# An expert's accumulating transfers by column blocks into four tables, and small constants made later

## What is computed

```python
def moe(xn, w_router, wg, wu, wd):
    ...
    top_vals, top_idx = lax.top_k(logits, TOP_K)
    gates = jax.nn.softmax(top_vals, axis=-1)
    comb = jnp.einsum('nk,nke->ne', gates, jax.nn.one_hot(top_idx, N_EXPERTS, dtype=jnp.float32))
    y = jnp.zeros_like(t)
    for e in range(N_EXPERTS):
        y = y + comb[:, e:e + 1].astype(t.dtype) * swiglu(t, wg[e], wu[e], wd[e])
    return y.reshape(B, S, D)
```

## Time and profile before

| | |
|---|---|
| runs, median | 1997.23 us |
| runs, lowest and highest | 1994.70 and 1999.85 us |
| the profiled execution | 1999.13 us |
| its span in the profile | 1997.2 us, mean granted clock 0.986 |
| TensorE busy | 1936.9 us (97%) |
| VectorE busy | 1358.9 us (68%) |
| ScalarE busy | 1182.9 us (59%) |
| POOL busy | 99.3 us (5%) |
| DMA | 513.45 MB, mean 257 GB/s |

### The profile page before, as it was taken

One profiled execution on the slowest core, in us unless ns is written; L12 is line 12 of the kernel. 1 busy time (PEld: TensorE's weight loads), 2 busy tenths in 40 slices (PEclk: granted clock), 3 DMA queues, 4 the chain that ended last, 5 costly groups with the idle time before them and its releaser, 6 DMA issues.

```text
span 1997.2 us, 27157 instructions
## 1 busy us (share of the span) xinstructions
PE 1936.9 (97%) x9170; PEld 1614.0 (81%) x9170; DVE 1358.9 (68%) x1616; ACT 1182.9 (59%) x1501; POOL 99.3 (5%) x126
## 2 busy tenths in 40 slices
PE   9889999999999999999998989999999999999998
PEld 8778888888888888888887878878787878787876
DVE  8666654544554454546666668889798979788887
ACT  7666543434434343435555657878687878777775
POOL 8300000000000000000200000000000000000000
PEclk9999999999999999999998989999999999999999
DMA  9444566666566666666654459999999999999996
GB/s 353 145 134 149 178 189 186 192 193 189 185 190 190 190 190 191 191 187 186 188 168 135 160 201 363 364 382 366 376 363 379 362 379 360 381 359 385 354 392 256
DMA packets 139251, 513.45 MB, mean 257 GB/s; under 512 B 15648, under 2 KB 15664, under 8 KB 136464
## 3 DMA queue, kind: packets, MB, share of 16 engines
q1 hardware_dynamic: 135440, 488.74, 70.7%
q0 software_dynamic: 3712, 23.44, 4.0%
HBM read 497.43 MB, written 14.69 MB: 256 GB/s over the span
## 4 chain that ended last, share of the span: by engine, by line
PE 82%; DMA 7%; ACT 3%; DVE 3%; POOL 2%; issue 2%; SPq 0%; ACTq 0%; DVEq 0%; POOLq 0%
PE main L599 26%; PE main L601 25%; PE main L600 25%; DMA raw_pieces<-in_ffn_moe 7%; ACT w_high L1031 1%; DVE w_low L1364 1%; PE transpose L927 1%; PE transpose L970 1%; PE transpose L617 1%; PE transpose L798 0%; PE transpose L910 0%; PE spread L661 0%; DVE heads_scratch L1412 0%; DVE small L1413 0%; PE transpose L639 0%
## 5 line engine op out<-in xcount | busy, mean ns | idle before, releaser
L1364 DVE TENSOR_TENSOR w_low<-raw_pieces,w_high 128x1024 fp32r<-128x1024 f32 x919 | 1095.5, 1225 | 469.4 <-ACT w_high L1031 465.1
L1031 ACT ACTIVATE w_high<-raw_pieces 128x1024 fp32r<-128x1024 f32 x919 | 944.9, 1058 | 280.5 <-DMA raw_pieces<-in_ffn_moe 142.2
L599 PE MATMUL main<-w_high,xT_high 128*128 128x512 f32 (+1 forms) x1920 | 738.1, 384 | 1.4 <-DVE x_resid L1562 1.0
L601 PE MATMUL main<-w_high,xT_low 128*128 128x512 f32 (+1 forms) x1920 | 725.8, 378 | 0.0
L600 PE MATMUL main<-w_low,xT_high 128*128 128x512 f32 (+1 forms) x1920 | 725.5, 378 | 0.0
L601 PEld LDWEIGHTS main<-w_high,xT_low 128*128 128x128 f32 x1920 | 364.6, 190 | 67.9
L599 PEld LDWEIGHTS main<-w_high,xT_high 128*128 128x128 f32 x1920 | 366.0, 191 | 65.7 <-issue 2.4
L600 PEld LDWEIGHTS main<-w_low,xT_high 128*128 128x128 f32 x1920 | 365.7, 190 | 63.7
L599 PE MATMUL main<-w_high,hT_high 128*128 128x512 f32 x832 | 329.2, 396 | 0.7 <-DVE hT_low L1771 0.7
L601 PE MATMUL main<-w_high,hT_low 128*128 128x512 f32 x832 | 324.6, 390 | 0.0
L600 PE MATMUL main<-w_low,hT_high 128*128 128x512 f32 x832 | 324.2, 390 | 0.0
(11 more groups left out here) (248 smaller groups left out, 883.8 us busy)
## 6 DMA issues: line engine op xcount, KB each, us to landing
raw_pieces<-in_ffn_moe SPq DMA_DIRECT2D x528, 512.0 KB, 5.6
raw_pieces<-in_ffn_dense SPq DMA_DIRECT2D x264, 512.0 KB, 3.7
raw_pieces<-in_w_in SPq DMA_DIRECT2D x96, 512.0 KB, 3.7
raw_pieces<-in_w_out SPq DMA_DIRECT2D x32, 512.0 KB, 3.6
residual_rows<-x_resid POOLq DMA_DIRECT2D x3, 1024.0 KB, 6.2
x_resid<-in_x SPq DMA_DIRECT2D x4, 512.0 KB, 14.7
xn_rows<-token_major POOLq DMA_DIRECT2D x2, 1024.0 KB, 5.1
x_resid<-residual_rows POOLq DMA_DIRECT2D x4, 512.0 KB, 7.6
```

What stands on the lines that cost most here:

```text
L599: pe.matmul(out_ap, lh[ls], rh[rs], start=first, stop=False)
L601: return pe.matmul(out_ap, ll[ls], rh[rs], start=False, stop=last)
L1031: act.activation(WH[:, piece % RING, :], RAWS[:, piece % RING, :], ACT.Copy).then_inc(high_done, 1)
L1364: dve.tensor_tensor(WL[:, piece % RING, :], RAWS[:, piece % RING, :], WH[:, piece % RING, :], ALU.subtract).then_inc(low_done, 1)
```

## The change

Two parts. The table becomes four tables of 384 x 512, one for each column block, with a semaphore each, and the one accumulating transfer of an expert becomes four, each issued when its block of `Y` is done. The table's first filling goes by columns as well (4 writes of 512 KB and 4 of 256 KB in place of 3 of 1 MB), and the gathers no longer wait for `y_out`. VectorE's wait at step 8 is for all four semaphores. The second part takes the eight small instructions of `TOKEN`, `PLACE` and `VAL` out of `masks()` and puts them behind `rope_tables(0)`.

```diff
-        RESULTS = nc.dram_tensor("residual_rows", (SEQ + SLOTS, D), F32, kind="Internal").ap()
+        RESULTS = [nc.dram_tensor(f"residual_rows{d}", (SEQ + SLOTS, NB), F32, kind="Internal").ap() for d in range(DBLOCKS)]
...
-        x_out, y_out = sem("residual_stored"), sem("y_out")
+        x_out, y_out = sem("residual_stored"), [sem(f"y_out{d}") for d in range(DBLOCKS)]
...
             def masks():
                 link(pool.tensor_copy(IOTA[:, :], IOTA_I))
-                pool.wait_ge(token_iota, 2)
-                link(pool.tensor_copy(TOKEN[:, :], TOKEN_I[:, :]))
-                link(pool.tensor_copy(PLACE[:, 0:1], PLACE_I[:, :]))
-                link(pool.tensor_scalar(PLACE[:, 1:2], PLACE[:, 0:1], -1.0, None, ALU.mult))
-                link(pool.tensor_scalar(PLACE[:, 2:3], PLACE[:, 0:1], float(SEQ), None, ALU.add))
-                for t in range(TILES):
-                    link(pool.memset(VAL[:, t, 2, :], 1.0))
-                    ins = pool.tensor_scalar(VAL[:, t, 0, :], VAL[:, t, 2, :], TOKEN[:, t:t + 1], None, ALU.mult)
-                ins.then_inc(token_done, 1)
                 link(pool.tensor_copy(DF, DIST))
...
             rope_tables(0)
 
+            pool.wait_ge(token_iota, 2)
+            link(pool.tensor_copy(TOKEN[:, :], TOKEN_I[:, :]))
...
+            ins.then_inc(token_done, 1)
+
             pool.wait_ge(used, MIX[1]["piece"])
...
             pool.wait_ge(dn_free, FFN[1]["dn"])
-            for t in range(TILES):
-                pool.dma_start(RESULTS[t * P:(t + 1) * P, :], X[:, t, :]).then_inc(x_out, 16)
-            pool.dma_start(RESULTS[SEQ:SEQ + SLOTS, :], X[:, 0, :]).then_inc(y_out, 16)
-            pool.wait_ge(x_out, 16 * TILES)
-            pool.wait_ge(y_out, 16)
+            for d in range(DBLOCKS):
+                pool.dma_start(RESULTS[d][0:SEQ, :].rearrange("(t p) n -> p t n", p=P),
+                               X[:, :, d * NB:(d + 1) * NB]).then_inc(x_out, 16)
+            for d in range(DBLOCKS):
+                cols = slice(d * NB, (d + 1) * NB)
+                pool.dma_start(RESULTS[d][SEQ:SEQ + SLOTS, :], X[:, 0, cols]).then_inc(y_out[d], 16)
+            pool.wait_ge(x_out, 16 * DBLOCKS)
             for e in range(N_EXP - 1):
                 pool.wait_ge(idx_done, e + 2)
                 pool.indirect_dma_start(XG, None, ROWS[:, :], bass.IndirectOffsetOnAxis(ap=IDX[:, 0:1], axis=0)).then_inc(xg_in, 16)
 
 
-                pool.wait_ge(y_out, 16 * e + 16)
                 pool.wait_ge(cur_done, e + 1)
-                pool.wait_ge(dn_free, PASS[0]["dn"] + DBLOCKS * (e + 1))
-                pool.indirect_dma_start(RESULTS[:, :], bass.IndirectOffsetOnAxis(ap=RC[:, 0:1], axis=0), Y, None,
-                                         compute_op=ALU.add).then_inc(y_out, 16)
+                for d in range(DBLOCKS):
+                    cols = slice(d * NB, (d + 1) * NB)
+                    pool.wait_ge(y_out[d], 16 * e + 16)
+                    pool.wait_ge(dn_free, PASS[0]["dn"] + DBLOCKS * e + d + 1)
+                    pool.indirect_dma_start(RESULTS[d][:, :], bass.IndirectOffsetOnAxis(ap=RC[:, 0:1], axis=0), Y[:, cols], None,
+                                            compute_op=ALU.add).then_inc(y_out[d], 16)
...
-            pool.wait_ge(y_out, 16 * N_EXP)
+            for d in range(DBLOCKS):
+                pool.wait_ge(y_out[d], 16 * N_EXP)
...
                         if i == E_SELECT and not direct:
 
-                            dve.wait_ge(y_out, e * 16 + 16)
+                            for d in range(DBLOCKS):
+                                dve.wait_ge(y_out[d], e * 16 + 16)
                             dve.tensor_copy(GC[:, :], GN[:, :])
```

More of the change, by code:

```diff
@@ L548, in _ @@
             rope_tables(0)
+            pool.wait_ge(token_iota, 2)
+            link(pool.tensor_copy(TOKEN[:, :], TOKEN_I[:, :]))
+            link(pool.tensor_copy(PLACE[:, 0:1], PLACE_I[:, :]))
+            link(pool.tensor_scalar(PLACE[:, 1:2], PLACE[:, 0:1], -1.0, None, ALU.mult))
+            link(pool.tensor_scalar(PLACE[:, 2:3], PLACE[:, 0:1], float(SEQ), None, ALU.add))
+            for t in range(TILES):
+                link(pool.memset(VAL[:, t, 2, :], 1.0))
+                ins = pool.tensor_scalar(VAL[:, t, 0, :], VAL[:, t, 2, :], TOKEN[:, t:t + 1], None, ALU.mult)
+            ins.then_inc(token_done, 1)
             pool.wait_ge(used, MIX[1]["piece"])
@@ L591, in _ @@
                 pool.dma_start(X[:, :, d * NB:(d + 1) * NB],
-                               RESULTS[0:SEQ, d * NB:(d + 1) * NB].rearrange("(t p) n -> p t n", p=P)).then_inc(back_in[d], 16)
+                               RESULTS[d][0:SEQ, :].rearrange("(t p) n -> p t n", p=P)).then_inc(back_in[d], 16)
         @block.tensor
```

## The result

The changed kernel takes 1963.14 us, the median of four runs (1961.98 to 1965.02); the kernel before, run beside it, takes 1996.01 (1994.70 to 1999.85). The ratio is 0.9833 with a 95% interval from 0.9816 to 0.9850: 33 us less (29.9 to 36.7). The forecast was 1969.0 with a range from 1964 to 1988, so the sign is right, the gain is 4 us more than the 29.2 of the sum, and the time is 0.9 us outside the range.

A forecast was written before the change was run, and what follows sets the result against it. TensorE was taken to set the pace, stalling once per expert when one late 1 MB accumulating transfer delays weights. Savings 18.0 + 8.3 + 2.9 = 29.2 us from 1999.13 give 1969.9, from the median 1968.0; forecast 1969, range 1964 to 1988.

The forecast's parts named there:

- slow stretches: Experts: after six of the gaps TensorE runs at its lower clock; removing these saves 6 x 1.38 = 8.3 us.
- seven gaps, 18.0 us: Experts, second onward: TensorE's stalls of 2.15 to 3.11 us before the first transpose all go, saving 18.0 us.
- The experts as a whole: Experts: gaps and slow stretches together were forecast to save 26.3 us.
- The small constants: Kernel start: moving eight instructions shortens POOL's chain before ScalarE's sine; all 2.9 us comes through, bounds 2.4 and 2.9.
- small gaps of 0.48 us: Last transpose of an expert: left in the forecast; if gone too, 7 x 0.48 = 3.4 us toward the range's lower end.
- Lag and cover: First transpose of the next expert: weights' lag of 0.3 to 1.3 us stays inside 1.2 to 2.2 us covered by pieces made ahead.
- Rival (a): Experts: gaps stay in part, through leftover lag or smaller packets alternating with weights; gain 13 to 21 us, 1978 to 1986; 18%.
- 92.3 us, with 2.8 us to spare: One expert's DMA work: pieces 84.2, gather 2.8, four quarters 5.3 us, fitting within 95.1 us.
- POOL's issues and the filling: POOL: 21 more issues and five more table-filling issues, 1.71 us each, fit in its idle time and cost nothing.
- The rule against the change: Experts' transfers: if the skill's 2.0 us fixed per DMA filled the engines, four cost 10.4 us against 4.4 for one.
- rival (c): Experts: each transfer's fixed time fills the DMA engines; 2033 us, or 1993 by the skill's fit; 3%.

The follow-up runs named there:

- 1: Kernel before with only the eight small instructions moved behind the rope tables; 1992.54 us, ratio 0.9978 to the kernel before.
- 2: Changed kernel with the eight small instructions put back into `masks()`, leaving four tables and four transfers alone; 1969.59 us, ratio 0.9868 to the kernel before.
- 5: Changed kernel run again, unaltered; 1962.91 us, ratio 0.9826 to the kernel before.
- 9: Changed kernel without the move of the small constants, run a second time; 1969.16 us, ratio 0.9859 to the kernel before.
- 4: Kernel before without the seven accumulating transfers, first seven experts' results left out of the sum; 1967.58 us, ratio 0.9858 to the kernel before.
- 3: Changed kernel with each of the four transfers waiting for the expert's last block; 1982.18 us, ratio 0.9930 to the kernel before.
- 6: Changed kernel with two tables of 1024 columns and two transfers, after the second and fourth block; 1972.73 us, ratio 0.9876 to the kernel before.
- 7: Changed kernel with each expert's last quarter accumulated a second time, into a spare table; 1973.24 us, ratio 0.9884 to the kernel before.
- 11: Changed kernel with all four quarters of each expert accumulated a second time, into a spare table; 2012.64 us, ratio 1.0076 to the kernel before.
- 12: Changed kernel with two transfers of half the columns, both after the last block; 1993.52 us, ratio 0.9990 to the kernel before.
- experiment 10: Changed kernel with POOL's two small loads (frequencies, positions) issued in the middle of `masks()`; 1961.81 us, ratio 0.9830 to the kernel before.
- experiment 8: Changed kernel with POOL's angles and their loads ahead of the rest of `masks()`; 1969.16 us, ratio 0.9859 to the kernel before.

## Why the prediction was right, and where it was not

**The gaps and the slow stretches: right, the second a little small.** The step "seven gaps, 18.0 us" measured 18.1, from 23.5 to 5.4 us of idle time. The experts as a whole gave 27.4 us: to the end of the span they take 807.9 to 810.1 us with the old transfer (before, 1) and 780.4 to 782.2 with four (changed, 2, 5, 9), means 809.0 and 781.6; by the ratios of 2 and 9 it is 26.3 and 28.1. Forecast 26.3. The slow stretches were then worth 27.4 - 18.1 = 9.3 us for 8.3 forecast, if all that remains is put down to them.

**The small constants: the step that failed.** The term "all of it comes through: 2.9" with bounds 2.4 and 2.9 measured 4.4 alone and 6.8 beside the four transfers. The wait before the sine fell as forecast, from 5.43 to 2.45, and the sine came 2.9 us earlier (52.39 to 49.47). But the experts start 5.1 us earlier: at 1185.2 us in the mean of four kernels with the constants unmoved (before, 2, 4, 9: 1183.7 to 1187.1), at 1180.1 in the mean of eight with them moved and nothing else changed at the start (changed, 1, 3, 5, 6, 7, 11, 12: 1177.1 to 1182.5). From the scatter of these twelve starts the 5.1 is known to some 2.6 us. 27.4 + 5.1 = 32.5 us, where 32.9 were measured.

The other 2.2 us go with the granted clock of the mixers. Half of them are there early: TensorE's first transpose of `h_blocks` in the dense part of layer 0 stands at 255.2 us in the mean of the four and at 251.2 in that of the eight, 4.0 us earlier. Where the lead grows from 2.9 to 4.0 shows in the 12 us from 60 on, for the kernel before, the changed kernel and the changed kernel again (the clock is the third number from the end):

```profile
60.00:72.00 12.00, 6.40 (x26) 5.31 (x26) 7.92 (x10) 6.18 (x10) 7.09 (x11) 0.86 0.26 67
```

```profile
60.00:72.00 12.00, 9.81 (x40) 7.75 (x40) 5.69 (x7) 7.45 (x11) 6.96 (x15) 0.86 0.35 113
```

```profile
60.00:72.00 12.00, 9.72 (x46) 7.86 (x45) 7.15 (x10) 9.03 (x13) 7.25 (x15) 1.00 0.44 141
```

With the constants unmoved TensorE waits 4.75 to 5.60 us just before, and the clock of these 12 us is 0.72 to 0.86 in all four. With them moved it waits at most 2.48 us, and the clock is 0.86 in four kernels (changed, 1, 3, 6) and 1.00 in the other four (5, 7, 11, 12). The same kernel shows both, so a gap of this length is followed by the lower clock in some executions and not in others. The later stages differ as well. Two stretches of each, of the kernel before and then of the changed one:

```profile
1050.00:1100.00 50.00, 43.96 (x194) 36.14 (x193) 33.10 (x56) 28.11 (x40) 0.00 (x0) 0.90 0.43 128
1150.00:1200.00 50.00, 44.09 (x257) 37.79 (x257) 33.63 (x79) 28.49 (x56) 2.65 (x5) 0.90 0.55 200
```

```profile
1050.00:1100.00 50.00, 45.29 (x216) 37.77 (x217) 35.44 (x63) 27.23 (x38) 0.00 (x0) 0.97 0.44 134
1150.00:1200.00 50.00, 44.09 (x263) 37.79 (x262) 35.31 (x77) 29.48 (x55) 6.10 (x10) 0.93 0.60 213
```

Of the stretches of 50 us that I read, from 55 to 305 and from 1000 to 1200, four have a clock under 1.00: 55 to 105, 105 to 155, 1050 to 1100 and 1150 to 1200. Summed over these, the missing part (1 less the clock) times 50 us is 13.5 to 15.5 us in the four unmoved kernels and 8.5 to 12 in the eight moved ones; the two groups don't overlap. The prediction took a shift of the start as a shift of everything behind it. It had seen that the clock falls behind gaps in the experts, and did not ask what it does behind those in the mixers. Near 64 us the shorter gap goes with the fewer slow stretches. Why an earlier angle leaves fewer of them a thousand microseconds later isn't shown; no experiment here tried it, and it stays open. So does why experiment 10, where TensorE waits 1.5 us less at the start (0.73 for 2.19), doesn't end sooner.

**The range and the base.** Two terms were small, this one by 2.2 us and the experts by 1.1. The lower end of the range held nothing for either: below the forecast it had only the small gaps of 0.48 us, most of which stayed, and the spread of the runs. Part of the 0.9 us outside is also the base. The 1969 was counted mostly from a profiled execution of 1999.13 us. From the 1996.01 that the kernel before took beside the changed one, the same sum gives 1966.8.

**Lag and cover: right in size, wrong in one argument.** The prediction had 0.3 to 1.3 us of lag against a cover of 1.2 to 2.2. ScalarE's wait was 1.30 us and TensorE's gap nil. Rival (a) counted it as a danger that smaller packets alternate with the weights and make a lag last longer. They do alternate; but experiments 3 and 12 show that this is a gain, since the lag that comes late does no harm before the first transpose (experiment 3 paid for some of it in its last expert).

**"92.3 us, with 2.8 us to spare": wrong, without effect.** Experiments 7 and 11 put the need at 93.9 to 96.6 us. The sum took each piece at its best rate, 1.28 us, and the results at 5.3 us, for 5.9 measured. Which of the other terms holds the rest wasn't measured. One quarter more (experiment 7) already cost 10 us, so a change that added DMA work would have been misjudged by this step.

**POOL's issues and the filling: right.** The four issues of the expert shown took 1.55 to 1.61 us, and POOL then idled 31.22 us before the next gather. Experiment 4 has none of these issues, fills one table as before, and waits for no transfer at step 8; its experts take 781.0 us against 781.8 and 781.9, so all three together cost under 1 us.

**The rule against the change.** The Trainium skill, "DMA: Bandwidth & Descriptors", section "Rules for kernel authors", asks for at least 1 MiB in a DMA and for small transfers to be put together. By that rule the change would have lost. The fixed time of its fit fell with rival (c). Here the runs show the reverse: 4 x 256 KB beat 2 x 512 KB by 10 us (experiment 6) and 1 x 1 MB by 26 to 28. The Trainium skill has on the same page, in the section "Queues, rings and completion order", the rule that bears on it: each engine serves its queues in turn, a packet of several descriptors at a time. The nearly equal counts of experiments 3 and 12 agree with turns; what the profile counts as a packet is a single row (144 for a transfer of 128 rows, with 16 small ones), so how many rows make a turn isn't shown.

## What to carry to other kernels

When a large transfer competes with a stream of weights that is nearly full, look at when it runs and at how long its packets are, not at its bytes: cut it so that parts go as soon as they are done, and so that what must go late is small and in short packets, because the stream keeps its share by packets. Find the stream's true margin by adding a little work to it, not by summing best rates. And price a shift at the start not only by its length, but also by the clock of the stages behind it, with a range for it where executions differ.

## What the runs showed of the hardware that was not expected

- An accumulating transfer costs the engines by its bytes: about 590 ns for a packet of 8 KB, 64.3% x 6 us x 16 / 214 = 288 ns for 4 KB (experiment 12), 50.1% x 10 us x 16 / 500 = 160 ns for 2 KB (experiment 3). Small rows carry no extra price here.
- In the experts the seven gaps of 0.60 to 1.60 us of experiment 3 are not followed by a lower clock, while those of 2.15 us and more in the kernel before are in six of seven cases; the one at 1312.86, of 3.05 us, isn't. The length alone doesn't decide: a gap of 1.98 us in experiment 12 was followed by the lower clock, and gaps of 2.07 (experiment 6), 2.42 (experiment 1) and 2.89 us (experiment 12) were not.
- POOL's instructions on 128 x 384 elements slow VectorE's subtraction with two inputs from 1.23 to 1.71 us in the mean of six (7.38 and 10.27 us). The Trainium skill, "SBUF — State Buffer", section "Who interferes with whom", says that a VectorE instruction with two inputs in SBUF contends with a GpSimd instruction that reads SBUF; experiment 8 agrees and gives the price.
- The DMA traffic, nearly all of it weights read from HBM, holds 409 GB/s on one core over 22 us of the changed kernel, at a DMA share of 1.02.
